# Feed-forward weight pairs on Trainium2: a new order of gates and downs, later parts of inner values, and weight sums over a copy in PSUM

## The reference, cut to what matters

```
h = h + 0.5 * swiglu(rms_norm(h, ffn1_norm), ffn1_w_in, ffn1_w_out)
h = h + hybrid_mixer(rms_norm(h, mix_norm), ...)
h = h + 0.5 * swiglu(rms_norm(h, ffn2_norm), ffn2_w_in, ffn2_w_out)
def swiglu(h, w_in, w_out):
    gate, up = split(h @ w_in)          # 1024 -> 2 x 2816
    return (silu(gate) * up) @ w_out    # 2816 -> 1024
```

## Time and profile before

| | |
|---|---|
| median of the runs shown | 3662.39 us (3660.53 to 3664.61, 3 runs) |
| the profiled execution | 3664.31 us, of which the span from the first to the last instruction is 3662.5 us |
| mean granted TensorE clock | 0.979 |
| busy share of the span | PE 92%, PEld 79%, DVE 61%, POOL 47%, ACT 44% |
| the four feed-forward runs | from 979.4, 1952.1, 2339.8 and 3276.5 us on |

### The profile page before, as it was taken

One profiled execution on the slowest core, in us unless ns is written; L12 is line 12 of the kernel. 1 busy time (PEld: TensorE's weight loads), 2 busy tenths in 40 slices (PEclk: granted clock), 3 DMA queues, 4 the chain that ended last, 5 costly groups with the idle time before them and its releaser, 6 DMA issues.

```text
span 3662.5 us, 64634 instructions
## 1 busy us (share of the span) xinstructions
PE 3385.5 (92%) x23756; PEld 2903.8 (79%) x23756; DVE 2233.5 (61%) x4178; ACT 1599.5 (44%) x2976; POOL 1737.3 (47%) x1316
## 2 busy tenths in 40 slices
PE   8999997999589999999999999899999999999997
PEld 6766875333489988989798999899987887779897
DVE  5645455111588786243658878888874335578877
ACT  4333221111445555333635455555554335455554
POOL 3322442323267761424045777577752333257775
PEclk9999998999799999999999999999999999999998
DMA  3211226997222221222032222222221322122222
GB/s 130 75 49 46 91 97 246 351 350 276 97 97 93 93 98 41 96 81 87 24 104 70 104 100 87 80 104 99 98 87 42 103 73 81 36 93 105 91 104 81
DMA packets 98768, 390.50 MB, mean 107 GB/s; under 512 B 22416, under 2 KB 23248, under 8 KB 77392
## 3 DMA queue, kind: packets, MB, share of 16 engines
q1 hardware_dynamic: 80576, 367.82, 28.1%
q10 hardware_dynamic: 4112, 10.78, 0.9%
q0 software_dynamic: 13824, 8.44, 0.7%
HBM read 437.29 MB, written 16.78 MB: 124 GB/s over the span
## 4 chain that ended last, share of the span: by engine, by line
PE 57%; POOL 12%; DVE 10%; issue 9%; DMA 5%; ACT 4%; DVEq 2%; SPq 0%; POOLq 0%; ACTq 0%
PE ps L1358 16%; PE ps L831 14%; PE ps L835 7%; PE ps L847 5%; PE ps L1196 4%; DMA cs<-in_wp 4%; PE ps L977 2%; PE ps L995 2%; DVEq L2031 2%; PE ps L1206 2%; POOL merged L3214 2%; POOL front_lo L3226 2%; POOL w_lo L3198 2%; POOL fourth_lo L3226 2%; POOL back_lo L3226 2%
## 5 line engine op out<-in xcount | busy, mean ns | idle before, releaser
L3198 POOL TENSOR_TENSOR w_lo<-raw,w_hi 128x512 fp32r<-128x512 f32 (+1 forms) x448 | 577.5, 1311 | 1115.7 <-ACT w_hi L1483 1115.6
L1483 ACT ACTIVATE w_hi<-raw 128x1024 fp32r<-128x1024 f32 (+1 forms) x224 | 233.8, 1045 | 636.8 <-PE ps L835 475.1
L831 PE MATMUL ps<-hid_hi,w_hi 128*128 128x264 f32 (+2 forms) x1392 | 365.0, 318 | 0.0
L831 PE MATMUL ps<-hid_lo,w_hi 128*128 128x264 f32 (+2 forms) x1392 | 362.2, 316 | 0.0
L3226 POOL TENSOR_TENSOR front_lo<-merged,front_hi 128x512 fp32r<-128x512 f32 (+1 forms) x204 | 305.4, 1511 | 31.6 <-ACT front_hi L1761 31.6
L1358 PE MATMUL ps<-fast_hi,front_hi 128*128 128x264 f32 (+1 forms) x1056 | 273.0, 289 | 33.8 <-DVE fast_lo L2805 26.0
L1358 PE MATMUL ps<-fast_lo,front_hi 128*128 128x264 f32 (+1 forms) x1056 | 271.8, 288 | 0.0
L831 PEld LDWEIGHTS ps<-hid_hi,w_hi 128*128 128x128 f32 x1392 | 230.8, 188 | 19.5 <-issue 1.0
L831 PEld LDWEIGHTS ps<-hid_lo,w_hi 128*128 128x128 f32 x1392 | 230.9, 188 | 17.1
L835 PE MATMUL ps<-hid_hi,w_lo 128*128 128x264 f32 (+2 forms) x1392 | 232.8, 316 | 0.4 <-POOL w_lo L3198 0.4
L1358 PEld LDWEIGHTS ps<-fast_hi,front_hi 128*128 128x128 f32 x1056 | 202.9, 192 | 36.5 <-DVE fast_lo L2805 17.0
(11 more groups left out here) (580 smaller groups left out, 10342.8 us busy)
## 6 DMA issues: line engine op xcount, KB each, us to landing
raw<-in_w SPq DMA_DIRECT2D x206, 512.0 KB, 3.3
qb<-in_wp SPq DMA_DIRECT2D x68, 1024.0 KB, 4.8
merged<-in_wp SPq DMA_DIRECT2D x68, 512.0 KB, 3.2
cs<-in_wp SPq DMA_DIRECT2D x68, 512.0 KB, 4.1
e_hid_hi<-in_wexp SPq DMA_DIRECT2D x24, 1024.0 KB, 6.0
e_hid_lo<-in_wexp SPq DMA_DIRECT2D x24, 1024.0 KB
merged<-in_wexp SPq DMA_DIRECT2D x16, 1024.0 KB, 6.9
e_h_lo<-in_wexp SPq DMA_DIRECT2D x16, 1024.0 KB
```

The source lines that it names most:

```text
L831: pe.matmul(ps[:, 2 * b + bank, 0:m], wh, v[:, at:at + m], start=(k == 0 and i == 0), stop=False)
L1483: act.activation(w_hi[:, slot, 0:width * P], raw[:, slot, 0:width * P], ACT.Copy).then_inc(hi_done, 1)
L3198: ins = pool.tensor_tensor(w_lo[:, slot, cols], raw[:, slot, cols], w_hi[:, slot, cols].bitcast(F32), ALU.subtract)
```

## The change

Three things are done at once.
1. `PLAN` puts the next group's first gate ahead of a group's four downs, so that a down of group 0 or 1 follows a gate, an up follows the downs, and only group 2's first down follows its up. The weight stream is laid out in the same order.
2. In a pair behind an up, unless it is group 2's first down (`late`), the high and low parts of the up's inner values no longer stand in front of the Q addition: the first low part goes behind it, the second behind the V addition, the third to the pair's end. ScalarE's order is moved to match, with `fifth_copied` ahead of the next pair's A11. A gate's kept C21 and the chunk work of the closing downs go behind the Q addition too. GpSimd makes A12's low part ahead of `sum_one`.
3. ScalarE copies the raw A11 into S2's place in PSUM (`first_copy`). VectorE then makes S3 = copy - A21, S2 = A22 - S3 over the copy, and S4 = A12 - S2. S2 no longer needs S1, and ScalarE takes S2's high part only when S4 is done. The pairs at the head of a run that isn't chained to the one before (`opening`) are done as before.

In the diff below, `edge_copied`, `fifth_copied`, `quarter_begun` and `fifth_added` are the old lines of the W copy, the fifth copy and the Q and V additions as functions, and `first_variant` is the old L2855.

```diff
 PLAN = []
 for _g, _units in enumerate(GROUPS):
-    PLAN += [(_kind, _g, _j) for _j in range(_units // 2) for _kind in (GATE, UP)]
+    PLAN += [(_kind, _g, _j) for _j in range(_units // 2) for _kind in (GATE, UP)][_g > 0:]
+    PLAN += [(GATE, _g + 1, 0)] * (_g + 1 < len(GROUPS))
     PLAN += [(DOWN, _g, _j) for _j in range(DC // 2)]
...
         def chained(number):
             return number % PAIRS < PAIRS - 1 or number // PAIRS == CHAINED
+
+        def opening(number):
+            return number == 0 or not chained(number - 1)
+
+        def copies(number):
+            return sum(not opening(k) for k in range(number + 1))
...
                 elif i not in RAW:
-                    act.wait_ge({S1: s_one, S2: s_two, S3: s_three, S4: s_four}[i], number + 1)
+                    act.wait_ge({S1: s_one, S2: s_two if opening(number) else s_four, S3: s_three, S4: s_four}[i], number + 1)
...
+            def first_copy(number):
+
+                act.wait_ge(pair_in[number % 2], 16 * (1 + number % 2) * (number // 2 + 1))
+                act.wait_ge(pair_lo_dve, 3 * (number - 1) + 1)
+                act.wait_ge(s_four, number)
+                act.activation(s_bank(number, S2), pair_raw(number, RAW[A11]), ACT.Copy).then_inc(first_copied, 1)
...
                     first, more = i == 0, chained(number)
                     before = PLAN[i - 1][0] if i else None
                     closes = g == len(GROUPS) - 1 and kind == DOWN
-                    if before == UP:
+                    late = before == UP and kind == DOWN
+                    if late:
+                        first_copy(number + 1)
                         hidden_high(number - 1, 0, m)
-                    act.wait_ge(product_done, 7 * number + A11 + 1)
-                    if number:
-                        act.wait_ge(corner_taken, 4 * (number - 1) + C11 + 1)
-                    act.activation(ps[:, W_BANK, 0:m], ps[:, bank_of(number, EDGE), 0:m], ACT.Copy).then_inc(w_begun, 1)
+                        hidden_high(number - 1, 1, m)
+                    edge_copied(number, m)
...
-                    if before == UP:
-                        hidden_high(number - 1, 1, m)
+                    if late:
                         hidden_high(number - 1, 2, m)
+                    elif more:
+                        first_copy(number + 1)
+                    if i:
+                        pair_high(number, A22)
+                    if before == UP and not late:
+                        hidden_high(number - 1, 0, m)
+                    fifth_copied(number, m)
+                    if more:
+                        pair_high(number + 1, A11)
                     if before == GATE:
                         corner(number - 1, C21, m)
-                    if closes and j:
-                        chunks(number - 1)
-                    if i:
-                        pair_high(number, A22)
-                    if more:
-                        pair_high(number + 1, A11)
-                    act.wait_ge(product_done, 7 * number + S1 + 1)
-                    if number:
-                        act.wait_ge(v_added, number)
-                    act.activation(fifth_product[:, 0:m], ps[:, V_BANK, 0:m], ACT.Copy).then_inc(fifth_kept, 1)
                     if more:
                         pair_high(number + 1, S1)
                         pair_high(number + 1, S2)
+                    if closes and j:
+                        chunks(number - 1)
                     if kind == GATE:
                         corner(number, C11, m)
                     if more:
                         pair_high(number + 1, A12)
+                    if before == UP and not late:
+                        hidden_high(number - 1, 1, m)
                     if kind == GATE:
                         corner(number, C22, m)
                     if more:
                         pair_high(number + 1, S3)
+                    if before == UP and not late:
+                        hidden_high(number - 1, 2, m)
+                    if more:
                         pair_high(number + 1, S4)
                     if kind == GATE:
                         corner(number, C12, m)
...
                 if i == S3:
-                    ve.wait_ge(pair_in[number % 2], 16 * (1 + number % 2) * (number // 2 + 1))
-                    ve.tensor_tensor(s_bank(number, S3), pair_raw(number, 0), pair_raw(number, 1), ALU.subtract).then_inc(s_three, 1)
+                    if opening(number):
+                        ve.wait_ge(pair_in[number % 2], 16 * (1 + number % 2) * (number // 2 + 1))
+                        first = pair_raw(number, 0)
+                    else:
+                        ve.wait_ge(first_copied, copies(number))
+                        first = s_bank(number, S2)
+                    ve.tensor_tensor(s_bank(number, S3), first, pair_raw(number, 1), ALU.subtract).then_inc(s_three, 1)
+                elif i == S2 and not opening(number):
+                    settle()
+                    ve.tensor_tensor(s_bank(number, S2), pair_raw(number, RAW[A22]), s_bank(number, S3), ALU.subtract).then_inc(s_two, 1)
                 elif i == S2:
...
-                    if one == C12:
-                        v = v_staged(m)
-                        settle()
-                        ve.tensor_tensor(v[:, 0, :], v[:, 2, :], v[:, 1, :], ALU.subtract).then_inc(t_one, 1)
...
-                    if before is not None:
+                    if before == GATE:
+                        corner_kept(number - 1, C12, m)
+                    if i:
                         corner_begun(number - 1, C21, m)
-                    if before == UP:
+                    if late:
                         hidden_low(number - 1, 0, m)
+                        hidden_low(number - 1, 1, m)
                     settle()
                     if more:
-                        pair_sum(number + 1, S2)
-                    if before == UP:
-                        hidden_low(number - 1, 1, m)
+                        pair_sum(number + 1, S3)
+                    if late:
                         hidden_low(number - 1, 2, m)
-                    if before == GATE:
-                        corner_kept(number - 1, C12, m)
-                        corner_kept(number - 1, C21, m)
-                    if closes and j:
-                        chunks(number - 1)
                     if first:
                         ve.wait_ge(root_ready, step + 1)
-                    ve.wait_ge(product_done, 7 * number + S2 + 1)
-                    ve.wait_ge(fifth_kept, number + 1)
-                    settle()
-                    ve.tensor_tensor(ps[:, Q_BANK, 0:m], edge, fifth_product[:, 0:m], ALU.add).then_inc(q_begun, 1)
+                    quarter_begun(number, m)
                     if first:
                         ve.reciprocal(inverse[:, 0:m], inverse[:, 0:m])
+                    if more:
+                        pair_sum(number + 1, S2)
+                        pair_sum(number + 1, S4)
+                    if before == GATE:
+                        corner_kept(number - 1, C21, m)
+                    if before == UP and not late:
+                        hidden_low(number - 1, 0, m)
+                    if closes and j:
                         settle()
-                    else:
-                        if more:
-                            pair_sum(number + 1, S3)
-                            pair_low(number + 1, S2)
-                            pair_sum(number + 1, S4)
-                        corner_begun(number, C11, m)
-                    ve.wait_ge(product_done, 7 * number + S3 + 1)
-                    ve.tensor_tensor(v_at, edge, fifth_product[:, 0:m], ALU.add).then_inc(v_added, 1)
+                        chunk(2 * (j - 1))
+                    settle()
                     if first:
+                        fifth_added(number, m)
                         corner_begun(number, C11, m)
                         ve.reciprocal(inverse[:, m:n], inverse[:, m:n])
+                    else:
+                        corner_begun(number, C11, m)
+                        fifth_added(number, m)
                     settle()
                     corner_begun(number, C22, m)
-                    corner_kept(number, C11, m)
-                    if first:
-                        pair_sum(number + 1, S3)
+                    if more:
                         pair_low(number + 1, S2)
-                        pair_sum(number + 1, S4)
+                    if kind == GATE:
+                        corner_kept(number, C11, m)
+                    if closes and j:
+                        chunk(2 * (j - 1) + 1)
+                    if before == UP and not late:
+                        hidden_low(number - 1, 1, m)
+                    if kind == GATE:
+                        corner_kept(number, C22, m)
+                    corner_begun(number, C12, m)
+                    if kind == UP:
+                        first_variant(m)
```

(25 more changed lines are left out.)

52 lines of the change are left out of this document (32 added, 20 removed).

## The result

The changed kernel takes 3547.57 us at the median of four runs (3541.41 to 3549.72), the kernel before 3663.5 in four; the ratio is 0.9677, with a 95% interval of 0.9655 to 0.9698. The prediction was 3579 in a range from 3552 to 3626: the direction was right, and the gain 31 us larger than forecast, just outside the range. The profiled execution took 3548.78 us (span 3547.0), 115.5 less than the one before.

A forecast was written before the change was run, and what follows sets the result against it. TensorE, busy 92% of the span, was taken as the bound, with only its gaps and clock to win. Terms -54 - 18 - 4 - 1 - 6 = -83; 3664.3 - 83 - 1.9 = 3579 us, range 3552 to 3626.

The forecast's parts named there:

- The walk of gate and up: Gate pairs behind an up and the following up: additions in time, 20 us lost against 70 and 4, so -54 us.
- addition for contention: Gates behind an up: inner low parts colliding with GpSimd lose between 0 and 1.0 us each, taken as 0.5.
- Queues: GpSimd makes A12's low part before its own sum, no longer idling there for a load; no added load, no gain priced.
- first downs of groups 0 and 1: With a gate ahead of them, these feed-forward downs lose 9 us instead of 27: -18 us.
- group 0's later downs: They lose 10 us in 12 pairs; GpSimd's sum leaves VectorE's path: -4 us.
- closing downs: Chunk work moves from in front of Q to in front of V; only the last down gets free: -6 us.
- group 2's first downs: Still follow their up, with the same chain from C12 through the first variant to the low part: 0.
- The sums: S3 and S2 over a copy in PSUM take 0.70 us each: 1.3 us less VectorE work in a 512-wide pair.
- First and second pair: At a feed-forward run's head, the second pair gains from fewer low parts ahead, the first loses 0.5: -1 us.
- Free of it: Rival: the 0.7 us in hand always suffices in gates behind an up; 3559, or 3553 at best; chance 0.09.
- The waits move on: Rival: inner low parts hit GpSimd each time, a gate with its up loses 1.2 us; 3613 us, chance 0.22.
- ScalarE's copy waited for no load: Rival on ScalarE's queue: its copy waits for a load in each pair, slower at 3700 us; chance 0.05.

The follow-up runs named there:

- e13: The changed kernel with GpSimd's old order alone put back, its own sum ahead of A12's low part and the variants: 3566.0 us, ratio 0.9741.
- e15: The changed kernel run once more, unaltered: 3549.2 us, ratio 0.9684.
- e3: The changed kernel with S3 and S2 from SBUF, no copy into PSUM, and GpSimd's first sum waiting for S2 as before: 3587.6 us, ratio 0.9793.
- e8: The changed kernel with the first inner low part computed twice in each of the 40 gates behind an up: 3584.8 us, ratio 0.9765.

## Why the prediction was too small, by its own steps

**The walk of gate and up was right, its addition for contention was not.** Q was to come at 4.65 us and V at 7.9; in the pair shown they came at 4.61 and 8.07, the up's Q at 4.93 instead of 4.65. The forecast put 0.5 us of loss on each of 40 gates, 20 us, as half of an unknown. Measured: 3.8 us in the gates and 1.5 in the ups, so the term is -69 (74.0 to 5.3), not -54.

**The step that failed is the one under "Queues": GpSimd "no longer idles there for a load", priced at nothing.** I found the inner parts late through the chain from ScalarE's high part to GpSimd, and credited the whole remedy to the additions that no longer stand behind them. I did not follow the chain one link further, to the load that GpSimd waits for, though the row says 129.4 us of idle time. Without that order the change loses 98 (e13): a gain of 87 where the forecast had 83, with 14.6 lost in gates and ups where it had 20. So the sum was nearly that of the change without GpSimd's order, and the order adds the 19 us that it lacked (17 by the times of e13 and e15). Alone it does 66. In part this nearness is luck: in e13 the gates with the ups (-59 for -54) and the first downs of groups 0 and 1 (-18 for -18) came as forecast, while the pairs at a run's head (-7 for -1) and group 0's later downs (-7 for -4) made up for closing downs (+1 for -6) and group 2's first downs (+5 for 0).

Of the 31 us by which the forecast fell short, 23 lie inside the runs (105.8 against 83). The other 8 are those ahead of the runs, for which the sum had no term; without them the time would be some 3556 us, inside the range. Whether they belong to the change stays open, as said above.

**The sums were underrated too.** In the forecast they shortened VectorE by 1.3 us a pair and took GpSimd's sum off the path of group 0's later downs, -4; these went from 10.4 to 0.9. Taken out of the change they cost 35 us (e3). That they free GpSimd as well, 1450 to 1281 ns over all 544 low parts, was no term of the sum: contention was counted as a cost to VectorE only.

**Smaller terms.** First downs of groups 0 and 1: -18 forecast, 27.3 to 6.6 measured, -21; the first run's one lost 6.0 against 5.5. First and second pair: -1 forecast, 26.6 to 20.8, -6: the second pairs, 13.8 before, lose 3.7, while the first pairs got worse by 4.3 in all. Closing downs: -6 forecast, -2.3; the 1.8 us per down of the first and third run came as walked, and V leads the waits behind the runs' heads. Group 2's first down: 0 forecast, 2.6 worse, but 2.0 better in e15, so no more than scatter.

**The rivals.** "Free of it" gave 3553 to 3559 and had 0.09. Its picture of the gates came true (5.3 us lost with the ups), through GpSimd's order: without that, in e13, the loss is near the forecast's. Its time too was short, by the terms above. "The waits move on" did not come; its low parts did get longer (median 1.09 instead of 0.98 us), and e8 shows that some 0.4 us more per gate would have begun to make it true. Of the rule that the prediction quoted beside it ("SBUF — State Buffer" in the Trainium skill, Who interferes with whom), the runs bear out the pairing: GpSimd's low parts, which read SBUF, take 1.41 to 1.51 us on average in the six versions with both sums from SBUF and 1.28 to 1.34 in the eleven with neither. They bear out the hold as well. In the gate pair of the earlier trace rows, VectorE's sum from SBUF (1012.21 + 1.65) ends 0.57 us after GpSimd's variant (1011.51 + 1.78) that was at work when it began. In the changed kernel 63 inner parts of 128x528 begin beside a GpSimd instruction; the 60 that find more than 0.15 us of it left all end 0.56 to 0.57 us after it. So such a part is held for what is left of the other's instruction, and a walk that sets the two queues side by side could have priced the contention that the prediction took as half of an unknown.

ScalarE's copy waited for no load (0.0 us idle ahead of it). The 65 ns that "Perfetto Trace Analysis" in the Trainium skill (Optimizing Scalar/DVE Operations) puts on VectorE's PSUM access do not show: S3 with one operand in PSUM has 700 ns at the median, as much as the sums with two operands in SBUF had at the shortest.

**The range.** The bounds of the terms together run from -115 to -37, and the -106 inside the runs lies within them. The range's low end, 3552, took the best case of the gates and the closing downs alone. A term held to be zero has no best case: GpSimd's order had none, and neither had the stretch ahead of the runs. The forecast's own band is also misworked: half of the bounds' spread gives 3563 to 3602, not 3558.

## What to carry to other kernels

Where an in-order queue holds an instruction that waits for a load, list what stands behind it and who waits for that, and price the move of every such instruction, however small the diff: here one instruction moved behind another was worth more alone than any other part. Follow a late operand to its last link, past the engine that is seen waiting. And before adding gains of several parts, ask whether they remedy the same lateness: these four give 66, 41, 15 and -7 us alone, and 106 together.

## What was not expected of the hardware

A copy by ScalarE from SBUF into PSUM (128x512) took 0.60 us, its conversions of that size 0.62 from SBUF into SBUF and 0.60 from PSUM. VectorE's sums over PSUM (S3, L2822) took 0.70 us in every pair of 512 columns, whatever GpSimd did beside them. Of VectorE's two sums, one with two SBUF operands took GpSimd's low parts from 1281 to 1387 ns on average, two took them to 1508. The start of the first run, behind the stretch that is paced by loads, moved by up to 19 us between profiles (969.3 to 988.3, over 18 profiles), more than several of the effects looked for: the sum of the windows told versions apart that the whole time did not.
